# Gated linear attention heads: key gate folded into the exponents of levels and state, last two level rounds between the halves of the next value panel

## The reference

```
f = lb + (1.0 - lb) * sigmoid(f_pre)
k, lf = 1.0 - f, log(f)                       # per direction, forward and backward
b = cumsum(lf)
o = einsum('bhtk,bhkv->bhtv', q * exp(b), S)  # S: state of the context tokens
a = q . (exp(b_t - b_s) * k_s)  for s <= t    # per key channel
o = o + a @ v
S = einsum('bhsk,bhsv->bhkv', k * exp(b_last - b), v)   # context tokens give the first S
```

## Time and profile before

| | |
|---|---|
| median of 3 runs | 2500.62 us (2497.35 to 2502.97) |
| the profiled execution, its own time | 2495.28 us |
| its span in the trace | 2493.6 us |
| mean granted clock of PE in it | 0.962 |
| PE busy | 2310.1 us, 93% of the span |
| DVE busy | 1737.6 us, 70% |
| ACT busy | 1110.3 us, 45% |

### The profile page before, as it was taken

The page is one execution under the profiler, slowest core; times in us unless marked ns, Lnnn a source line. Parts: engine busy times, 40 slices in busy tenths (PEclk is TensorE's granted clock), DMA queues, the critical chain, the costliest instruction groups (busy, mean ns, idle before and its releaser), DMA issues.

```text
span 2493.6 us, 37876 instructions
## 1 busy us (share of the span) xinstructions
PE 2310.1 (93%) x13692; PEld 1997.0 (80%) x13692; DVE 1737.6 (70%) x3390; ACT 1110.3 (45%) x1761; POOL 86.1 (3%) x140
## 2 busy tenths in 40 slices
PE   7999899997999889996999999999988999999968
PEld 7998679987998679995777778888867888888858
DVE  7777857777787858875455554444545999999984
ACT  4343443344433443334555543334334656555652
POOL 0000000000000000002121101110100000000000
PEclk9999889998999989998999999999998999999989
DMA  7654136554554135544343621221212222222212
GB/s 277 223 194 164 60 141 214 196 188 161 212 200 160 68 112 187 215 170 90 69 72 72 101 68 60 76 68 60 84 43 76 79 81 72 79 84 84 84 42 101
DMA packets 81765, 298.62 MB, mean 120 GB/s; under 512 B 10132, under 2 KB 10644, under 8 KB 80916
## 3 DMA queue, kind: packets, MB, share of 16 engines
q1 hardware_dynamic: 77904, 284.72, 32.4%
q0 software_dynamic: 2048, 4.20, 3.0%
q10 hardware_dynamic: 1736, 8.67, 0.9%
HBM read 296.51 MB, written 1.05 MB: 119 GB/s over the span
## 4 chain that ended last, share of the span: by engine, by line
PE 34%; DVE 13%; ACT 4%; issue 2%; DVEq 0%; ACTq 0%
PE ps L710 27%; DVE wsplit L1955 2%; DVE work L2629 2%; DVE work L2659 2%; DVE work L2680 1%; DVE work L2621 1%; PE ps L1161 1%; ACT work L1901 1%; PE ps L1043 1%; PE ps L1057 1%; ACT wsplit L1349 1%; PE ps L1033 1%; DVE work L2604 1%; DVE work L2602 1%; PE ps L1013 1%
## 5 line engine op out<-in xcount | busy, mean ns | idle before, releaser
L710 PE MATMUL ps<-hsplit,wsplit 128*128 128x256 f32 (+1 forms) x8280 | 1381.7, 325 | 26.8 <-DVE hsplit L2297 11.6
L710 PEld LDWEIGHTS ps<-hsplit,wsplit 128*128 128x128 f32 x8280 | 1202.1, 192 | 161.3 <-DVE wsplit L1955 16.0
L1955 DVE TENSOR_TENSOR wsplit<-ring,wsplit 128x1024 fp32r<-128x1024 f32 x465 | 575.5, 1240 | 264.0 <-ACT wsplit L1349 253.7
L1349 ACT ACTIVATE wsplit<-ring 128x1024 fp32r<-128x1024 f32 x465 | 491.0, 1058 | 598.3 <-PE ps L710 416.1
L752 PE MATMUL ps<-wsplit,fsplit 128*128 128x512 f32 x1056 | 264.1, 400 | 19.6 <-DVE wsplit L1955 14.2
L752 PEld LDWEIGHTS ps<-wsplit,fsplit 128*128 128x128 f32 x1056 | 197.5, 193 | 58.7 <-DVE wsplit L1955 14.9
L2003 DVE SCALAR_TENSOR_TENSOR work<-ring,cs,work 128x128 f32<-128x128 f32 x672 | 206.0, 348 | 9.0
L2109 DVE SCALAR_TENSOR_TENSOR work<-work,vec 128x256 f32<-128x256 f32 x240 | 100.9, 479 | 1.7
L1446 ACT ACTIVATE work<-ps 128x256 f32<-128x256 f32 x88 | 33.7, 383 | 152.1 <-PE ps L710 152.1
L710 PEld LDWEIGHTS ps<-wsplit,hsplit 128*128 128x128 f32 x768 | 96.1, 198 | 5.3 <-issue 3.8
L710 PE MATMUL ps<-wsplit,hsplit 128*128 128x256 f32 x768 | 97.7, 290 | 1.1 <-DVE wsplit L1955 1.1
(11 more groups left out here) (322 smaller groups left out, 2354.3 us busy)
## 6 DMA issues: line engine op xcount, KB each, us to landing
ring<-panels SPq DMA_DIRECT2D x539, 512.0 KB, 4.2
work<-latent_weights ACTq DMA_DIRECT2D x2, 2304.0 KB, 12.9
work<-rpb POOLq DMA_DIRECT2D x64, 64.0 KB, 6.6
cst<-constants ACTq DMA_DIRECT2D x1, 1408.0 KB
work<-x SPq DMA_DIRECT2D x1, 1024.0 KB, 5.3
work<-post_rows ACTq DMA_DIRECT2D x2, 512.0 KB, 4.2
cT<-ctx ACTq DMA_DIRECT2D x1, 1024.0 KB, 7.3
out<-xT SPq DMA_DIRECT2D x1, 1024.0 KB, 3.9
```

Source lines behind the costliest of these rows:

```text
L710: ins = mm(out_, w(a), x(b), start=start and n == 0, stop=stop and n == 2, **kw)
L1349: af(wsplit[:, split_slot(name, n), 0, :], ring[:, p % slots, :], ACT.Copy).then_inc(high_ready, 1)
L1955: tt(parts[:, 1, :], ring[:, p % slots, :], parts[:, 0, :].bitcast(fp32), ALU.subtract)\
```

## The change

The key gate is no longer a factor of its own. Its exponent `c_x` is added to the cumulated decay: `c_bx = c_b + c_x`, one DVE operation of 128x1024. The key side of the levels subtracts `c_bx` in place of `c_b`, and so do the state keys' exps on ACT. The eight products on DVE (L2659) and the product of the state keys (L2637) go. ACT's exp of the key gate is made only for the latent half that the diagonal needs (128x512 in place of 128x1024). ACT now signals `c_kh_ready` and `c_k_ready`.

On PE the value panel of the next head is cut in two halves, and rounds 2 and 3 are put between them: rounds 0 and 1, first half of the value panel, rounds 2 and 3, second half. PE gets three waits more: on `c_ro_ready` before the transposes, `c_y_ready` before the state product, `c_kd_ready` before the cross product.

```diff
-        c_kk = take(2, 2 * T)
+        c_bx = take(2, 2 * T)
+        c_kl = take(2, T)
...
@@ PE
-                    if heads_done is not None:
+                    if heads_done is not None and half == 0:
                         pe.wait_ge(c_v_ready, heads_done)
-                    full_panel("C", n0 + 4, ps[:, 3, :], i)
+                    half_panel("C", n0 + 4, ps[:, 3, :], i, half)
...
                 pe.wait_ge(c_kh_ready, h + 1)
+                if before:
+                    pe.wait_ge(c_ro_ready, h)
...
                 pe.wait_ge(c_v_ready, h + 1)
+                if before:
+                    pe.wait_ge(c_y_ready, h)
...
                 pe.wait_ge(c_k_ready, h + 1)
+                pe.wait_ge(c_kd_ready, h + 1)
...
                 for r in range(4):
+                    if nxt and r == 2:
+                        c_project(*nxt, 3, h + 1, 0)
                     if r >= 2:
                         pe.wait_ge(c_lev_read, h * 4 + (r - 1))
...
                 if nxt:
-                    c_project(*nxt, 3, h + 1)
+                    c_project(*nxt, 3, h + 1, 1)
...
@@ ACT
-                af(c_kk[:, :, :], c_x[:, :, :], ACT.Exp, scale=-1.0)
+                af(c_kl[:, :, :], c_x[:, :, 0:T], ACT.Exp, scale=-1.0)
...
-                A.did(af(c_kh[:, 0, :], c_b[:, 0, T:2 * T], ACT.Exp, scale=-1.0, bias=c_b[:, 0, 2 * T - 1:2 * T]))
-                af(c_kh[:, 1, :], c_b[:, 1, T:2 * T], ACT.Exp, scale=-1.0, bias=c_b[:, 1, T:T + 1]).then_inc(c_w_ready, 1)
+                act.wait_ge(c_w_ready, h + 1)
+                A.did(af(c_kh[:, 0, :], c_bx[:, 0, T:2 * T], ACT.Exp, scale=-1.0, bias=c_b[:, 0, 2 * T - 1:2 * T]))
+                af(c_kh[:, 1, :], c_bx[:, 1, T:2 * T], ACT.Exp, scale=-1.0, bias=c_b[:, 1, T:T + 1]).then_inc(c_kh_ready, 1)
...
-                af(c_ak[:, :, :], c_ak[:, :, :], ACT.Exp).then_inc(c_ek_ready, 1)
+                af(c_ak[:, :, :], c_ak[:, :, :], ACT.Exp).then_inc(c_k_ready, 1)
...
@@ DVE
                 B_ = 2 * T
+                tt(c_bx[:, :, :], c_b[:, :, :], c_x[:, :, :], ALU.add).then_inc(c_w_ready, 1)
                 base = c_b[:, 0, :]
...
-                    own = at(base, 0, (2 * g, nb), (g + B_, 2), (1, g))
+                    own = at(c_bx[:, 0, :], 0, (2 * g, nb), (g + B_, 2), (1, g))
...
-                dve.wait_ge(c_w_ready, h + 1)
-                tt(c_kh[:, :, :], c_kk[:, :, T:2 * T], c_kh[:, :, :], ALU.mult).then_inc(c_kh_ready, 1)
...
-                V.did(tt(c_kd[:, :], c_kk[:, 0, 0:T], c_kk[:, 1, 0:T], ALU.add))
+                tt(c_kd[:, :], c_kl[:, 0, :], c_kl[:, 1, :], ALU.add).then_inc(c_kd_ready, 1)
...
-                dve.wait_ge(c_ek_ready, h + 1)
-                for lev, g in enumerate(LEVELS):
-                    nb = T // (2 * g)
-                    v = c_ak[:, lev, :].rearrange("p (n a g) -> p n a g", n=nb, a=2)
-                    ins = tt(v, at(c_kk[:, 0, :], 0, (2 * g, nb), (g + B_, 2), (1, g)), v, ALU.mult)
-                    if lev < 7:
-                        V.did(ins)
-                ins.then_inc(c_k_ready, 1)
```

More of the change, by code:

```diff
@@ L550, in build @@
         c_eq_ready = sem("c_eq_ready")
-        c_ek_ready = sem("c_ek_ready")
+        c_kd_ready = sem("c_kd_ready")
         c_q_ready = sem("c_q_ready")
@@ L1219, in _, with c_project @@
             norm(2, sq, after=(rstd_ready, R_FIRST + 2))
-            def c_project(n0, i, which, heads_done):
+            def c_project(n0, i, which, heads_done, half=None):
                 if which == 0:
@@ L1311, in _ @@
             pe.wait_ge(h_ready, H_FIRST + 32)
-            for which in range(4):
+            for which in range(3):
                 c_project(0, 0, which, None)
+            for half in range(2):
+                c_project(0, 0, 3, None, half)
             c_head(0, (5, 0), before=False)
@@ L2624, in c_head @@
                 ins.then_inc(c_aq_ready, 1)
+                dve.wait_ge(c_w_ready, h + 1)
                 for lev, g in enumerate(LEVELS):
                     nb = T // (2 * g)
-                    own = at(base, 0, (2 * g, nb), (g + B_, 2), (1, g))
+                    own = at(c_bx[:, 0, :], 0, (2 * g, nb), (g + B_, 2), (1, g))
                     border = at(base, g - 1, (2 * g, nb), (1 + B_, 2), (0, g))
@@ L2644, in c_head @@
                 tt(c_qz[:, 1, :], ps[:, 2, T:2 * T], c_s[:, 1, :], ALU.mult).then_inc(c_qz_ready, 1)
-                V.did(tt(c_kd[:, :], c_kk[:, 0, 0:T], c_kk[:, 1, 0:T], ALU.add))
+                dve.wait_ge(c_qz_sig, h + 1)
+                tt(c_kd[:, :], c_kl[:, 0, :], c_kl[:, 1, :], ALU.add).then_inc(c_kd_ready, 1)
                 dve.wait_ge(c_qz_ready, h * 2 + 2)
```

## The result

The changed kernel takes 2538.83 us (median of 4 runs, 2533.79 to 2545.83) against 2498.98 (4 runs, 2494.41 to 2502.97). The ratio is 1.0162, 95% interval 1.0127 to 1.0197: 1.6% slower, some 40 us. The profiled execution is the longest of the four, 2545.83 us, with a span of 2544.2.

What follows compares the result with a forecast made beforehand. A cycle through PE and DVE was taken to set the 32.84 us a head. Losses of 29.6 us, or 41.4 with the falling clock, gave 2536.7 from the profiled run and 2542 from the median; 2540 was written, range 2522 to 2565.

Steps and rivals of the forecast that it cites:

- Leg one: PE's stretch from the start of gate panel 2 until DVE can read round 2: from 18.37 to 19.65 us.
- leg two: DVE's serial stretch from reading round 2 to the end of gate panel 2's low: from 14.41 to 15.56 us.
- The filled wait: Half the value panel, 2.87 us, fills PE's 1.59 us wait before round 2 but takes longer than it.
- c_bx: The added DVE operation between scans and subtractions lengthens leg two by 1.15 us a head, bounds 1.1 and 1.25.
- The later round: Round 2, behind half the value panel, is ready 1.28 us later after gate panel 2's start, lengthening leg one.
- The removed work: Dropping DVE's eight products and the state keys' product gains nothing in a middle head, at most 0.24 us.
- The sum with the clock up: A middle head needs 35.27 us in place of 32.84, 2.43 more, before any cost of a fallen clock.
- The clock: PE's clock falls behind 3.5 us waits in three in five of 14 heads, 1.4 us each, 11.8 us.
- in every head and for long: Rival on PE's clock: it falls in all 14 heads with the long stretch, +60.4 us, 2561; chance 0.16.
- Head 0 to 1: First step between heads: PE doesn't wait for DVE at gate panel 2, so only round 2's delay counts, +1.28 us.
- Head 14 to 15: Step into the final head: c_bx adds 1.15 us, the vanished wait before round 2 takes 1.59, together -0.4.
- the last head: Nothing hides DVE there; without the eight products PE's cross product starts 2.9 us sooner.

Runs made afterwards that it cites:

- e3: The changed kernel with 12 more matmuls of 512 columns on PE in each of heads 1 to 14, ahead of the mean's wait: 2522.4 us.
- e11: The kernel before with only rounds 2 and 3 put between the value panel's halves, plus 9 added matmuls a head (1 to 14) ahead of the mean: 2504.0 us.
- e1: The kernel before with only PE's order changed, rounds 2 and 3 between the halves of the value panel: 2512.9 us.
- e7: The changed kernel with 15 added matmuls ahead of the mean's wait and c_bx computed twice, first into a tile nobody reads: 2539.3 us.
- e2: The changed kernel with all four rounds together ahead of the whole value panel, keeping the key gate in the exponents: 2504.7 us.
- e5: The changed kernel with only ACT's order made earlier, value's copy, high of gate panel 2 and square right behind the first exp: 2553.3 us.

## Why the prediction was right

**The two legs.** The mechanism is right, and its sizes are nearly so. Leg one was given as 19.65 us and is 19.24 with the clock up (e3), leg two 15.56 and is 15.54. The filled wait gave nothing, the half panel missing behind round 3 turned into waits of 3.6 to 3.9 us at the mean (forecast 3.5) and, with the clock up, 0.46 before gate panel 2 (forecast 0.7).

**c_bx.** Forecast 1.15 us, measured 1.13 by doubling it. In leg two entirely.

**The later round.** Forecast +1.28, measured +0.78 in e11: mis-sized, by two things. The idle time that the timeline gives before round 2, 1.59, counts from the end of the last matmul. But matmuls that follow without a hole start some 0.24 us before that end: in the changed kernel the half panel starts 2161.06 - 2159.35 = 1.71 us behind round 0, whose matmuls are given 1.95. From start to start the way from round 0 to round 2 grew from 2167.72 - 2164.18 = 3.54 to 2188.46 - 2183.90 = 4.56 us (e3), only 1.02. And round 2 that follows other matmuls is ready for DVE in 2189.58 - 2188.46 = 1.12 us, where it took 2169.00 - 2167.72 = 1.28 behind the hole. That is 0.87 in leg one.

**The removed work.** Forecast nothing, at most 0.24 in a middle head. Right, near that bound: the fold alone costs 0.87 us a step where c_bx alone costs 1.13, and with the split, where that 0.2 has no use, the fold costs 34.94 - 33.79 = 1.15.

**The sum with the clock up.** 2.43 forecast for a middle head, 1.93 measured in e3. The two legs' growth, 0.87 + 1.13 = 2.00, is the difference of the shorter steps, 34.83 - 32.84; the mean before holds one head in which the clock fell.

**The clock.** Too small by its frequency. I gave three heads in five a fall at 1.4 us each, 0.84 on average; all 14 had one, and the mean is 1.41 us (36.35 against 34.94). The frequency came from five waits of 3.0 to 3.7 us. The same trace, behind its start, has nine longer waits ahead of the section, of 4.2 to 8.2 us. Over the 5 us behind each the granted clock was 0.50 to 0.58, and ahead of seven of them it had been 1.00. Why the two lone waits of 3.4 and 3.5 us had no fall stays open. The rival "in every head and for long" was right about every head and not about the price of 2.2. A part of the low stretch lies within PE's wait: in 2138 to 2145 PE is busy 4.80 of 7 us. The Trainium skill's passage on waits between bursts (TensorE: Matmul & The Clock Gate, "HAM oscillation — how this bites in real kernels") says that each round starts slow; the changed kernel's trace agrees in 14 of 14 heads. The filled wait, e3, shows that it is the wait that brings it; in e1, with waits of 2.6 to 2.9 us, 10 of 14 heads had the fall.

**The sum.** 13 middle steps cost 43.3 us more (3.33 each), forecast 42.6 with the clock's share. Head 0 to 1 cost 1.8 (33.02 to 34.82), forecast 1.28. That step of the prediction is wrong: it counted only the later round there, but the second c_bx makes this step longer too, by its whole 1.13 us (34.83 in e3, 35.96 in e7), and so does the fold alone, by 0.69 (33.71 in e2). Head 14 to 15 gave back 0.24 (41.83 to 41.59), forecast 0.4. In the last head the cross product came 2.9 us sooner, as forecast. It starts at 2482.62, 15.23 us behind the first scan, where it was 2431.90 - 2413.79 = 18.11. The scan of the kernel before, then both rows of the changed one:

```profile
2413.79 0.69 DVE L2607 TENSOR_TENSOR_SCAN work<-work 128x256 f32<-128x256 f32 x1
```

```profile
2467.39 0.69 DVE L2618 TENSOR_TENSOR_SCAN work<-work 128x256 f32<-128x256 f32 x1
...
2482.62 1.22 PE L1289 MATMUL ps<-work 128*128 128x128 f32 x4 [1.68 <-DVE work L2663]
```

From the first start of the line to the end of the span that makes 41.9 us, forecast 41.4. That it comes so near is luck, as two errors cancel: with the clock up (e3) the same stretch is 22.2 us longer than before, forecast 29.6, and the clock adds 19.7, forecast 11.8. The profiled execution is longer by 50.6; the other 8.7 lie ahead of the section, whose first L2615 starts at 1917.2 and not at 1908.5, in code that is the same. The measured ratio, which rests on four executions of each kernel, gives 40 us.

**What the list of waits would have hidden.** It names the square on ACT for 64.8 us. At the low clock the square is indeed on the way that ends last, as gate panel 1 behind it runs slowly. But moving it (e5) made things worse, since the low of gate panel 2 stands 0.5 to 0.7 us behind it. A wait is worth only its distance to the next one.

## What to carry to other kernels

When two engines work on each other's results in turn, cut the cycle at two hand-overs and add each leg, serial work only. Work that is moved between the halves of a cover is taken from the far end of it: ask what the cover hid there before filling a hole in front. And shorten the serial leg first; the same split that cost 0.8 us a head here earned 0.6 once the operation that PE waits for had been put ahead of 5.5 us of work that nobody waited for yet, and the square and `high` on ACT with it.

## What the runs showed of the hardware

A wait of PE of 3.6 to 3.9 us in each head was followed by a low clock every time (changed kernel, 14 of 14), one of 2.6 to 2.9 us in most (e1, 10 of 14), one of 1.6 us in one of 15 (before). A wait of 4.5 us (e5) had 2.6 us of extra time in the 24 matmuls behind it. Twelve added matmuls per head that compute nothing of use made a kernel 16 us faster (e3).

The time ahead of the section moved between profiled executions from 1904.6 to 1917.2 us in code that is the same in all of them. PE's busy time in it went with that, from 1775.6 to 1789.8 us for the same 10499 matmuls. The stretches before the section's first L2604 or L2615, of the kernel before and then of the changed kernel:

```profile
0.00:1908.50 1908.50, 1777.74 (x10499) 1529.27 (x10500) 1240.98 (x2445) 789.54 (x1350) 86.09 (x140) 0.96 0.40 132
```

```profile
0.00:1917.20 1917.20, 1789.77 (x10499) 1538.99 (x10500) 1235.27 (x2445) 791.52 (x1350) 88.84 (x140) 0.95 0.40 132
```

The same instructions, 12 us more of busy PE at a clock of 0.95 in place of 0.96. What makes it fall more often in one execution than in another was not tried.
